# Sample attention: a third home for the cached values, and their loads requested one batch sooner

## The reference, cut to what matters

```python
k_all = jnp.concatenate([kv_past[:, :, 0].astype(k_a.dtype), k_a], axis=1)
v_all = jnp.concatenate([kv_past[:, :, 1].astype(v_a.dtype), v_a], axis=1)
...
for win, dil in DILATED_PATTERNS:
    ...
    s = jnp.einsum('bthd,btjhd->bhtj', q, kg).astype(f32) * scale + bias
    ...
    p = jnp.exp(s - mx)
    den = jnp.sum(p, axis=-1)
    o = jnp.einsum('bhtj,btjhd->bthd', p, vg.astype(f32)) / jnp.swapaxes(den, 1, 2)[..., None]
```

## Time and profile before

| | us |
|---|---|
| three timed runs | 2557.3, 2556.5, 2543.88 |
| their median | 2556.5 |
| the profiled execution, its own time | 2545.86 |
| its span, first to last instruction | 2544.1 |
| PE busy / DVE busy / ACT busy in the span | 2450.5 / 1571.9 / 1137.7 |
| granted TensorE clock, mean | 0.986 of full speed |

### The profile page before, as it was taken

How to read it: one execution, slowest core, us unless ns; L and a number is a source line. 1 busy time by engine, 2 the same in 40 slices (tenths; PEclk the granted TensorE clock), 3 DMA queues, 4 the chain that set the end, 5 groups by cost and what they waited for, 6 DMA issues and landing times.

```text
span 2544.1 us, 46062 instructions
## 1 busy us (share of the span) xinstructions
PE 2450.5 (96%) x16924; PEld 1409.8 (55%) x16924; DVE 1571.9 (62%) x3679; ACT 1137.7 (45%) x2680; POOL 322.3 (13%) x696
## 2 busy tenths in 40 slices
PE   7999987799999999999999999999999999999997
PEld 4557765467768586745544444444444444444543
DVE  6657876766767667678788755556655782121322
ACT  5458986544545454533365443333333452111211
POOL 1002220001112121211100112212200000000202
PEclk9999998999999999999999999999999999999999
DMA  6431335711111111154333444444422445434645
GB/s 226 136 106 51 107 107 155 225 41 35 36 44 27 52 52 62 44 184 147 116 93 95 120 130 136 125 137 133 143 82 71 116 133 187 165 137 171 173 150 97
DMA packets 274919, 289.15 MB, mean 114 GB/s; under 512 B 15549, under 2 KB 235720, under 8 KB 273280
## 3 DMA queue, kind: packets, MB, share of 16 engines
q1 hardware_dynamic: 264426, 251.52, 32.1%
q0 software_dynamic: 10272, 34.70, 5.2%
HBM read 191.20 MB, written 94.97 MB: 112 GB/s over the span
## 4 chain that ended last, share of the span: by engine, by line
PE 54%; DVE 2%; ACT 1%; issue 0%; POOL 0%; POOLq 0%; ACTq 0%; DVEq 0%
PE f_bank L3009 8%; PE f_bank L3010 8%; PE f_bank L3011 8%; PE f_bank L120 4%; PE f_bank L118 4%; PE f_bank L119 4%; PE f_banks_then_turned L3009 2%; PE f_banks_then_turned L3011 2%; PE f_banks_then_turned L3010 2%; PE f_bank_gate L118 1%; PE f_bank_gate L119 1%; PE f_bank_gate L120 1%; PE m_ps_then_y L118 1%; PE m_ps_then_y L120 1%; PE m_ps_then_y L119 1%; PE o_ps_y L118 1%
## 5 line engine op out<-in xcount | busy, mean ns | idle before, releaser
L118 PE MATMUL m_ps_then_y<-w_in_then_w_out_lo,act 128*128 128x256 bf16 x640 | 174.4, 273 | 0.1
L120 PE MATMUL m_ps_then_y<-w_in_then_w_out_lo,act 128*128 128x256 bf16 x640 | 174.4, 273 | 0.0
L119 PE MATMUL m_ps_then_y<-w_in_then_w_out_lo,act 128*128 128x256 bf16 x640 | 174.4, 273 | 0.0
L3009 PE MATMUL f_bank<-act,f_sums_and_w_then_down 128*128 128x512 bf16 x400 | 151.6, 379 | 0.6 <-DVE f_mid L3456 0.6
L3010 PE MATMUL f_bank<-act,f_sums_and_w_then_down 128*128 128x512 bf16 x400 | 151.6, 379 | 0.0
L3011 PE MATMUL f_bank<-act,f_sums_and_w_then_down 128*128 128x512 bf16 x400 | 151.6, 379 | 0.0
L2069 DVE SCALAR_TENSOR_TENSOR y_then_w_out<-z_then_patterns,m_hd,y_then_w_out 128x512 f32<-128x512 f32 x120 | 90.2, 752 | 79.8 <-ACT y_then_w_out L1803 77.0
L118 PE MATMUL m_ps_then_y<-act,w_in_then_w_out_lo 128*128 128x512 bf16 (+1 forms) x400 | 129.9, 343 | 5.4 <-DVE w_in_then_w_out_lo L2036 4.5
L119 PE MATMUL m_ps_then_y<-act,w_in_then_w_out_lo 128*128 128x512 bf16 (+1 forms) x400 | 129.8, 343 | 0.0
L120 PE MATMUL m_ps_then_y<-act,w_in_then_w_out_lo 128*128 128x512 bf16 (+1 forms) x400 | 129.3, 343 | 0.0
L3009 PE MATMUL f_bank<-mix_m_hi_then_tokens,f_sums_and_w_then_down 128*128 128x512 bf16 x320 | 121.3, 379 | 0.2 <-issue 0.2
(11 more groups left out here) (715 smaller groups left out, 7079.2 us busy)
## 6 DMA issues: line engine op xcount, KB each, us to landing
hidden_blocks<-f_h_block SPq DMA_DIRECT2D x66, 256.0 KB, 2.6
m_w_raw<-in_w_gate SPq DMA_DIRECT2D x30, 512.0 KB, 3.8
m_w_raw<-in_w_up SPq DMA_DIRECT2D x30, 512.0 KB, 3.9
f_t_then_hidden<-hidden_blocks SPq DMA_DIRECT2D x18, 704.0 KB, 5.5
f_hidden_then_hidden<-hidden_blocks SPq DMA_DIRECT2D x18, 704.0 KB, 5.5
hidden_blocks<-mix_m_hi_then_tokens SPq DMA_DIRECT2D x44, 256.0 KB, 2.6
hidden_blocks<-mix_m_lo_then_tokens SPq DMA_DIRECT2D x44, 256.0 KB, 2.9
act<-in_w_down POOLq DMA_DIRECT2D x22, 512.0 KB, 5.5
```

The costliest lines, as they stand in the source:

```text
L118: pe.matmul(out, w_hi, x_hi, start=first, stop=False, skip_group_check=in_parts)
L119: pe.matmul(out, w_hi, x_lo, start=False, stop=False, skip_group_check=in_parts)
L120: return pe.matmul(out, w_lo, x_hi, start=False, stop=last, skip_group_check=in_parts)
L3009: nc.tensor.matmul(bank[:, :], high, t_hi[q][j][:, kt, :], start=first and kt == 0, stop=False, skip_group_check=True)
```

## The change

1. **A third home.** Values have three homes, used by `b % 3`. The third is split: the two far tiles go to the idle `m_w_raw0`, the four near tiles to a new tile `s_v2_near`. It has a semaphore of its own, and `weigh_values` picks its rows from the far or the near part.
2. **One batch sooner.** V(b+1) is requested where V(b) was, and V(1) at the head of the stage, in front of the seven table loads. V(2) is requested where V(1) was. The new rows of a batch (L1046) keep two homes, have semaphores of their own (`new_in`) and stay where they were, except that those of batches 0 and 1 are issued together behind K(2).
3. **Order on PE and DVE.** PE turns the first key piece of batch 1 ahead of the tables, and DVE takes the tables over after `normalise(0, 0)` instead of before the first key copy of batch 1.
4. PE waits for two semaphores, `v_in` and `new_in`, where it waited for one.

```diff
-        v, v_new = [g.s_v0, sb("s_v1", [P, CACHE_TILES, D_A])], two("s_v_new", [DEC_SEQ, D_A])
+        whole = lambda tile: (tile[:, 0:FAR_TILES, :], tile[:, FAR_TILES:CACHE_TILES, :])
+        far2 = g.m_w_raw0[:, :, :].rearrange("p k c -> p (k c)")[:, 0:FAR_TILES * D_A].rearrange("p (t c) -> p t c", t=FAR_TILES)
+        v = [whole(g.s_v0), whole(sb("s_v1", [P, CACHE_TILES, D_A])), (far2, sb("s_v2_near", [P, CACHE_TILES - FAR_TILES, D_A])[:, :, :])]
+        V_SLOTS = len(v)
+        v_new = two("s_v_new", [DEC_SEQ, D_A])
...
                 def values(b):
-                    if b:
-                        cached_rows(sp, g, v[b % 2], v_in[b % 2], b, D_A)
-                    sp.dma_start(v_new[b % 2][:, :], g.v_sample[ds(b * DEC_SEQ, DEC_SEQ), :]).then_inc(v_in[b % 2], 16)
-
+                    cached_rows_in(sp, g, *v[b % V_SLOTS], v_in[b % V_SLOTS], b, D_A)
+
+                def new_values(b):
+                    sp.dma_start(v_new[b % 2][:, :], g.v_sample[ds(b * DEC_SEQ, DEC_SEQ), :]).then_inc(new_in[b % 2], 16)
+
+                values(1)
...
-                values(0)
...
                 keys(2)
-                values(1)
+                new_values(0)
+                new_values(1)
+                values(2)
...
                     sp.wait_ge(o_ready, b - 1)
-                    values(b)
+                    if b + 1 < DEC_BATCH:
+                        values(b + 1)
+                    new_values(b)
...
-                    hold(v_in[slot], (nth + 1) * (FAR_TILES + 2) * 16)
+                    hold(v_in[b % V_SLOTS], (b // V_SLOTS + 1) * (FAR_TILES + 1) * 16)
+                    hold(new_in[slot], (nth + 1) * 16)
...
                 scores(0, 0)
+                turn_k(1, 1, 0, 0)
                 turn_tables()
-                for pair in range(PAIRS):
+                for pair in range(1, PAIRS):
                     turn_k(1, 1, 0, pair)
...
                 mask_scores(0, 0)
-                keep_tables()
                 prepare(1, 1, [0])
                 normalise(0, 0)
+                keep_tables()
                 prepare(1, 1, range(1, PAIRS))
```

More of the change, by code:

```diff
@@ L185, in cached_rows, with cached_rows_in @@
 def cached_rows(queue, g, tile, loaded, b, first):
+    cached_rows_in(queue, g, tile[:, 0:FAR_TILES, :], tile[:, FAR_TILES:CACHE_TILES, :], loaded, b, first)
+def cached_rows_in(queue, g, far_to, near_to, loaded, b, first):
     cols = slice(first, first + D_A)
@@ L189, in cached_rows @@
     for f in range(FAR_TILES):
-        queue.dma_start(tile[:, f, :], far[f, :, 0:DEC_SEQ, :]).then_inc(loaded, 16)
+        queue.dma_start(far_to[:, f, :], far[f, :, 0:DEC_SEQ, :]).then_inc(loaded, 16)
     near = g.cache_kv[ds(b, 1), FAR:, cols].rearrange("o (t p) c -> p (o t) c", p=P)
-    queue.dma_start(tile[:, FAR_TILES:CACHE_TILES, :], near).then_inc(loaded, 16)
+    queue.dma_start(near_to, near).then_inc(loaded, 16)
 def stage_inputs_and_prompt_attention(nc, g, sems):
@@ L1005, in stage_sample_and_gates @@
         ps_new = ps_o[0:DEC_SEQ, O_FIRST * Q_TILES:(O_FIRST + 1) * Q_TILES]
-        (v_in1, k_turned, big_done, small_done, ready, s_ready, s_done, exp_done,
+        (v_in1, v_in2, new_in0, new_in1, k_turned, big_done, small_done, ready, s_ready, s_done, exp_done,
          rden_done, p_done, p_turned, p_kept, o_ready, o_kept, o_turned, o_hi, o_lo) = sems.new(
-            "s_v_in1", "s_k_turned", "s_big_done", "s_small_done", "s_new_ready", "s_s_ready", "s_s_done", "s_exp_done", "s_rden_done", "s_p_done", "s_p_turned", "s_p_kept",
+            "s_v_in1", "s_v_in2", "s_new_in0", "s_new_in1", "s_k_turned", "s_big_done", "s_small_done", "s_new_ready", "s_s_ready", "s_s_done", "s_exp_done", "s_rden_done", "s_p_done", "s_p_turned", "s_p_kept",
             "s_o_ready", "s_o_kept", "s_o_turned", "s_o_hi", "s_o_lo")
@@ L1014, in stage_sample_and_gates @@
             "g_log_w_done", "g_log_e_done", "g_own_done", "g_decay_ready", "g_tok_ready", "g_tok_done", "g_out_dma")
-        k_in, v_in = [g.s_k_in0, g.s_k_in1], [g.s_v_in0, v_in1]
+        k_in, v_in, new_in = [g.s_k_in0, g.s_k_in1], [g.s_v_in0, v_in1, v_in2], [new_in0, new_in1]
         prompt = lambda r: r[:, 0:SEQ].rearrange("h (s n) -> h s n", n=P)
@@ L1150, in turn_rows, with weigh_values @@
                                         g.ident[0:Q_TILES, 0:Q_TILES]).then_inc(o_turned, 1)
-                def weigh_values(slot, tiles):
+                def weigh_values(b, slot, tiles):
+                    far, near = v[b % V_SLOTS]
                     for tile in tiles:
                         n = P if tile < CACHE_TILES else DEC_SEQ
-                        rows = v[slot][:, tile, :] if tile < CACHE_TILES else v_new[slot]
+                        if tile < FAR_TILES:
+                            rows = far[:, tile, :]
+                        elif tile < CACHE_TILES:
+                            rows = near[:, tile - FAR_TILES, :]
+                        else:
+                            rows = v_new[slot]
                         for pair in range(PAIRS):
@@ L1185, in attend @@
                     hold(p_kept, b + 1)
-                    hold(v_in[slot], (nth + 1) * (FAR_TILES + 2) * 16)
-                    weigh_values(slot, range(CACHE_TILES // 3))
+                    hold(v_in[b % V_SLOTS], (b // V_SLOTS + 1) * (FAR_TILES + 1) * 16)
+                    hold(new_in[slot], (nth + 1) * 16)
+                    weigh_values(b, slot, range(CACHE_TILES // 3))
                     if more == 2:
                         turn_k(b + 2, slot, nth + 1, 1)
-                    weigh_values(slot, range(CACHE_TILES // 3, 2 * CACHE_TILES // 3))
+                    weigh_values(b, slot, range(CACHE_TILES // 3, 2 * CACHE_TILES // 3))
                     if more == 2:
                         turn_k(b + 2, slot, nth + 1, 2)
-                    weigh_values(slot, range(2 * CACHE_TILES // 3, CACHE_TILES + 1)).then_inc(o_ready, 1)
+                    weigh_values(b, slot, range(2 * CACHE_TILES // 3, CACHE_TILES + 1)).then_inc(o_ready, 1)
                     if b == DEC_BATCH - 2:
```

## The result

Over 20 runs of each, the changed kernel has a median of 2553.2 us (2544.28 to 2559.9) and the kernel before 2546.7 us (2541.39 to 2557.3). The ratio is 1.0022, with a 95% interval of 1.0012 to 1.0031: 3 to 8 us slower, where 1.05 us faster was forecast. The three runs shown ahead of the prediction had lain high; the median of 20 is 10 us lower. With two repeats among the experiments there are 44 runs of the changed kernel, mean 2552.2 us (standard error 0.6), against 172 of the kernel before, mean 2547.0 (0.3): 5.2 us slower.

The account below looks back on a forecast made before the run. PE, busy 96%, was taken to bound the kernel. Terms: -1.10 (batch 5's value wait), 0, 0, +0.05 (second semaphore wait) = -1.05 us, giving 2555.4 against the median 2556.5; range 2542 to 2559, 0.87 for within 0.5%.

Parts of the forecast that it names:

- The waits of batches 2, 3 and 5: PE's waits for values: removing those of batches 2 and 3 gains 0, that of batch 5 gains 1.10 us.
- The signs: Expected in the profile after, among others: `mask_scores` at unchanged distances up to batch 5, stage end 1.1 us sooner.
- Will the tables have landed?: Stage head: tables land behind V(1) at 433.3, needed at 434.02; cost taken as 0, at most 1.2 us.
- the signs named ahead for a wrong prediction: PE idle ahead of the tables, `g_soft` moved over 0.3 us, or `mask_scores` sooner in batches 2 to 4.
- Rival 2: Tables late at PE's `turn_tables`, delaying `g_soft` and DVE's chain: net +0.15 to +1.35 us; chance 0.20.
- The granted clock there is the lower of the two levels, and PE has as much to do as before, so I leave its rise where it is: Stage head, new order on PE: the clock's rise was left unmoved, and the sum on PE taken as 0.
- Is the third home fed in time?: Loads at the stage head: K(2) behind V(1) lands at 436, needed at about 441; cost 0.
- No PE wait for values in any batch: Sign expected in the profile after: PE waits for no values at L1159 in any batch.
- The range: Median of the changed kernel expected between 2542 and 2559 us, made from the spread of three runs of before.

Follow-up runs that it names:

- experiment 13: Changed kernel with the old PE/DVE order and loads requested in order of need (tables, keys, then values; new rows before next values): ratio 1.0002, stage 69.08 us.
- 12: The kernel before, unaltered, run again for a second profile: ratio 1.0006, stage 69.21 us.
- 10: The kernel before with only the three loads of V(1) moved in front of the seven table loads: ratio 1.0020, stage 75.87 us.
- experiment 2: The changed kernel with V(1) requested behind the seven table loads: ratio 1.0005, stage 70.60 us.
- 4: The changed kernel with PE turning the tables behind all key pieces of batch 1, and DVE taking them over later: ratio 1.0017, stage 72.72 us.
- 3: The changed kernel with V(1) requested behind the tables and the old order of work on PE and DVE: ratio 1.0002, stage 72.85 us.
- 7: The changed kernel with V(1) requested behind the tables, and the tables turned behind all key pieces of batch 1: ratio 1.0005, stage 72.40 us.
- experiment 11: The changed kernel with V(1) requested behind the tables and new rows ahead of the next batch's values, new order kept: ratio 1.0011, stage 72.85 us.
- experiment 5: The changed kernel with only the order on PE and DVE put back, V(1) still in front of the tables: ratio 1.0025, stage 76.33 us.
- 9: The changed kernel with V(1) behind the tables, the old PE/DVE order, and new rows ahead of the next batch's values: ratio 1.0013, stage 72.92 us.
- 15: The changed kernel with loads requested in order of need and tables turned behind all key pieces of batch 1: ratio 1.0016, stage 70.47 us.
- 6: The kernel before with only the new order of work on PE and DVE: ratio 1.0002, stage 72.29 us.
- 8: The kernel before with the tables turned behind all key pieces of batch 1 and taken over later by DVE: ratio 0.9998, stage 71.94 us.
- 16: The kernel before with the new rows of a batch issued ahead of its values: ratio 0.9994, stage 69.01 us.

## Why the prediction was wrong

**The waits of batches 2, 3 and 5: right.** The two that DVE hides were worth nothing, and the one of batch 5 was worth 1.10 us. The signs agree: from batch 1 to batch 4 the distances between `mask_scores` are those of before to 0.01 us. But the 1.10 is the worth in that one profile. The changed kernel's repeat kept a wait of 0.79 us there, and the kernels with two homes show 0.40 to 1.86. The worth of the third home at its best (experiment 13 against 12) is 69.21 - 69.08 = 0.13 us of stage, one profile of each.

**The step that failed: "Will the tables have landed?"** The term was taken as 0, from a landing at 433.3, with an upper end of 435.2 and 1.2 us of lateness. PE found the last table at 436.46 - 0.34 = 436.1, 2.1 us past the 434.02 at which it could use it. The near load took 8.1 us to land, not 6.3, the price of a load that I had read where a lone set of keys ran, and the tables came 1.6 us behind it, not 0.6: 1.8 and 1.0 us, which make the 2.8 from 433.3 to 436.1. The repeats have 7.2 and 8.2 us for the near load. Two of the signs named ahead for a wrong prediction came true: PE idled ahead of the tables, and `g_soft` moved by 1.76 us. Rival 2 had the place and the mechanism right, at a chance of 0.20, and a price too low: 1.35 us at most, where the change lost some 5 us, 2.8 of them to the tables by the count below.

**What the lateness cost.** Late tables cost time: moving V(1) in front of them is enough (10), and moving it back takes most of the loss away (2). They cost more than PE's wait. The step behind this is "The granted clock there is the lower of the two levels, and PE has as much to do as before, so I leave its rise where it is". It does not stay. In the twelve profiles with the tables in time, `mask_scores` of batch 1 follows the moment at which the clock is back, whatever the order and the number of homes: 14.73 to 15.12 us where that is 3.1 to 4.6, 16.42 to 16.75 where it is 8.5 to 9.3, 17.86 and 17.92 where it is 12.2 and 12.3. The three profiles of the changed kernel have the clock back at 8.7 to 9.3 and `mask_scores` at 18.78 to 19.62: 2.7 us later in the mean than the six profiles with that clock, for waits of 1.7 us in the mean. The rest fits the second stretch at 1.2 GHz, 7 us long, behind PE's stop. It is there in all three, and in experiments 4 and 10 from within the wait; in none of the twelve with the tables in time is the clock low again between 10 and 15 us. Behind the waits for keys in experiments 3 and 7 (3.49 and 1.25 us) it fell as well, for 3.4 and 3.5 us. From the first table transpose to `mask_scores` the changed kernel took 445.15 - 436.46 = 8.69 us, experiment 2, the same work without the second stretch, 7.69.

Not every stop does this: behind PE's wait of 1.82 us for keys in experiment 11 the clock stayed up for another 9 us. And in experiment 5, where the clock was still low, a wait of 3.36 us moved `mask_scores` by 3.4 us against 17.9, its own length.

The Trainium skill (TensorE: Matmul & The Clock Gate, What's actually happening) describes a gate that sets the clock by how busy the array has been recently. The trace agrees for the second stretch, which began within PE's stop or up to 2.0 us behind it; ahead of the stage, PE need not stand still for it: in the first profile of before the clock fell at 416.9, 4.6 us ahead of PE's idle time, PE having been busy for 0.68 of the 5 us up to 417. The same section of the Trainium skill says that the number of matmuls at the lower clock varies from run to run of one kernel; the trace agrees: the clock of the kernel before came back at 12.2 and at 4.6.

**Not all of the loss is the tables'.** The stage is 73.9 us long in the mean of three profiles of the changed kernel, and 71.1 in five of kernels with two homes and the tables in time: 2.9 us, about what `mask_scores` of batch 1 is late (3.0). The loss in time is some 5. The runs on record, put together after the fact, each kernel against the runs of before beside it, say where the rest may be (us slower in the mean, 95%):

| kernels | us slower than before |
|---|---|
| the changed kernel, three times | 5.0 (3.5 to 6.5) |
| third home, tables in time, seven kernels (2, 3, 7, 9, 11, 13, 15) | 2.2 (1.1 to 3.3) |
| two homes, tables in time, four kernels (6, 8, 12, 16) | 0.1 (-1.2 to 1.5) |

By this count late tables make 2.8 us of the loss (1.2 to 4.4), and the third home or its earlier requests some 2 us even with the tables in time. Rival 2 had only the first part. Over all runs with a recorded clock, (1 - mean granted clock) x span, the time that PE would lose if it were always busy, is 40.9 us for the changed kernel, 37.9 for the seven and 36.2 for before.

What remains open is why the third home costs some 2 us. PE's waits for keys in experiments 3, 7 and 11 are a part of the answer at most, since 9 and 15 have ratios of 1.0013 and 1.0016 without them. The stage does not show it: 71.6 us in the mean of the seven, 0.5 more than with two homes. It may be further stretches at the lower clock in the stages that follow. From the end of this stage to the last of the mLSTM's 256-column matmuls it took 557 to 567 us in profiles whose instructions there are the same, 562.0 in the mean of the seven and 561.2 with two homes. With single profiles I can't tell a systematic part from chance.

**"Is the third home fed in time?", half wrong.** The step said that keys of batch 2 a little later cost nothing. In the changed kernel PE waited for no keys, since late tables cover it. With the tables in time PE waited 1.25 to 3.49 us for them in three kernels out of five (3, 7 and 11, not 2 and 9): values stood in front of them. In the changed kernel itself they landed at 432.37 + 8.7 = 441.1, 5 us behind the estimate of 436. And the new rows, which stayed behind 1,152 KB of values in the queue, kept a wait of 0.5 to 1.0 us alive in batch 2 or 5 of all three profiles of the changed kernel. "No PE wait for values in any batch" was wrong for that reason; experiments 9, 11, 13 and 15, with the new rows first, have none. That it was not the values of batch 2 in the first profile the landing time shows: the near tiles, issued at 435.01, were there 10.3 us later, 15 us ahead of PE.

**The range** held the median, but only because the three runs that it was made from lay high: against them a loss of 5 us and a gain of 1 look alike. That is luck. The sign is what counts, and it was wrong.

No version tried is faster than the kernel before beyond its interval. The lowest is the kernel before with its new rows first, 0.9994 [0.9979, 1.0009], which is no difference.

## What to carry to other kernels

Before a large load is put in front of small ones, ask who needs the small ones first: on the one queue here they came in behind it, and their landing time was that of the large load, at the slow end of what the trace showed, plus their own. A third buffer helps only if the requests keep the order of need; here it let values pass keys, tables and new rows that were needed sooner. A stop of TensorE can cost more than its length: in five profiles here a wait of 1.4 to 4.9 us, with the clock back at 2.4 GHz or just coming back, was followed by 7 us at 1.2 GHz or ended in them. Where that can happen, a margin of under 1 us is not a margin. And before an effect of a few us is read from a stage, its clock has to be held against that of the other profile.

## What the runs showed that I had not expected

- One program, two profiles: the stage took 72.91 and 69.21 us, with the clock back 12.2 and 4.6 us behind its start. That spread of 3.7 us is three and a half times the effect that the change was reckoned to have.
- A load of 768 KB took 6.3 us to land in one place and 8.1 us in another (7.2 and 8.2 in the repeats), where only its own two far loads stood in front of it either; the tables behind the second needed 1.6 us more for some 0.16 MB.
- The DMA wait is named after the load issued last. In the kernel before it read as new rows; with these issued first it read as values and was still there.
